# The first eight transfers of a kernel, spread over the queues of SyncE and ScalarE

## What is computed

```python
def rmsnorm(x, g):
    xf = x.astype(jnp.float32)
    y = xf * lax.rsqrt(jnp.mean(xf * xf, axis=-1, keepdims=True) + EPS)
    return (y * g.astype(jnp.float32)).astype(x.dtype)

def first_block(x, c, ada_w, ada_b, pre_mix_g, ...):
    c_act = jax.nn.silu(c)
    for l in range(DEPTH):
        mod = c_act @ ada_w[l] + ada_b[l]
        sh1, sc1, ga1, sh2, sc2, ga2 = [m[:, None, :] for m in jnp.split(mod, 6, axis=-1)]
        h = rmsnorm(x, pre_mix_g[l]) * (1.0 + sc1) + sh1
        y = hybrid_mixer(h, w_in[l], ...)
        x = x + ga1 * rmsnorm(y, post_mix_g[l])
        h = rmsnorm(x, pre_ffn_g[l]) * (1.0 + sc2) + sh2
        y = swiglu_ffn(h, w_ffn_in[l], w_ffn_out[l])
        x = x + ga2 * rmsnorm(y, post_ffn_g[l])
    return x
```

## Time and profile before

| | |
|---|---|
| median of 3 runs | 1330.96 us (1330.03 to 1331.42) |
| the profiled execution's own time | 1328.96 us |
| its span, first to last instruction | 1327.1 us |
| outside its span | 1.86 us |
| TensorE busy | 1309.0 us, 99% of the span |
| transfers | 155.60 MB, mean 117 GB/s, all the kernel's own on one hardware queue |

### The profile page before, as it was taken

The page is one execution under the profiler, slowest core; times in us unless marked ns, Lnnn a source line. Parts: engine busy times, 40 slices in busy tenths (PEclk is TensorE's granted clock), DMA queues, the critical chain, the costliest instruction groups (busy, mean ns, idle before and its releaser), DMA issues. The chain is left out here.

```text
span 1327.1 us, 19480 instructions
## 1 busy us (share of the span) xinstructions
PE 1309.0 (99%) x7546; PEld 1150.7 (87%) x7546; DVE 1045.7 (79%) x1317; ACT 731.6 (55%) x1045; POOL 113.2 (9%) x86
## 2 busy tenths in 40 slices
PE   8999999999999999999999999999999999999997
PEld 6889888879989989989999897888888898889886
DVE  7899999999989689746849769997577876786663
ACT  4424888785546345534545856787365434443444
POOL 0000000012100591000012001010200000000001
PEclk9999999999999999999999999999999999999999
DMA  9634411167333433222252151301222232223212
GB/s 366 256 128 112 159 63 48 33 220 277 131 149 104 143 143 122 101 96 96 96 191 72 64 175 48 93 27 64 96 95 95 95 100 91 95 95 128 77 69 76
DMA packets 28731, 155.60 MB, mean 117 GB/s; under 512 B 3248, under 2 KB 5680, under 8 KB 15600
## 3 DMA queue, kind: packets, MB, share of 16 engines
q1 hardware_dynamic: 28656, 154.58, 33.4%
HBM read 145.39 MB, written 4.19 MB: 113 GB/s over the span
## 5 line engine op out<-in xcount | busy, mean ns | idle before, releaser
L2155 DVE TENSOR_TENSOR w_lo<-raw,w_hi 128x2048 fp32r<-128x2048 f32 (+3 forms) x139 | 249.4, 1796 | 47.0 <-ACT w_hi L1237 35.3
L1237 ACT ACTIVATE w_hi<-raw 128x2048 fp32r<-128x2048 f32 (+2 forms) x74 | 131.2, 1773 | 31.3 <-PE psum L920 15.4
L658 PE MATMUL psum<-h_hi,w_hi 128*128 128x512 f32 x360 | 92.1, 394 | 0.1
L658 PE MATMUL psum<-h_hi,w_lo 128*128 128x512 f32 x360 | 91.1, 391 | 0.0
L658 PE MATMUL psum<-h_lo,w_hi 128*128 128x512 f32 x360 | 90.4, 389 | 0.0
L658 PE MATMUL psum<-xg_hi,w_hi 128*128 128x512 f32 x336 | 83.0, 389 | 0.0
L658 PE MATMUL psum<-xg_hi,w_lo 128*128 128x512 f32 x336 | 83.0, 389 | 0.0
L658 PE MATMUL psum<-xg_lo,w_hi 128*128 128x512 f32 x336 | 83.0, 389 | 0.0
L658 PEld LDWEIGHTS psum<-h_lo,w_hi 128*128 128x128 f32 x360 | 67.6, 188 | 14.1
L658 PEld LDWEIGHTS psum<-h_hi,w_lo 128*128 128x128 f32 x360 | 67.0, 188 | 13.7
L658 PEld LDWEIGHTS psum<-h_hi,w_hi 128*128 128x128 f32 x360 | 66.0, 188 | 14.2 <-DVE w_lo L2155 0.7
(11 more groups left out here) (501 smaller groups left out, 3336.7 us busy)
## 6 DMA issues: line engine op xcount, KB each, us to landing
raw<-w_ffn_in SPq DMA_DIRECT2D x22, 1024.0 KB, 4.9
raw<-w_up SPq DMA_DIRECT2D x22, 1024.0 KB, 4.8
ada_first<-ada SPq DMA_DIRECT2D x16, 512.0 KB, 12.0
raw<-w_gate SPq DMA_DIRECT2D x8, 1024.0 KB, 4.9
raw<-w_mix_out SPq DMA_DIRECT2D x8, 1024.0 KB, 4.9
raw<-w_ffn_out SPq DMA_DIRECT2D x8, 1024.0 KB, 4.9
raw<-w_down SPq DMA_DIRECT2D x8, 1024.0 KB, 4.8
ada_x<-ada SPq DMA_DIRECT2D x11, 512.0 KB, 5.3
```

Source lines behind the costliest of these rows:

```text
L658: last = mm(ps, w[slot][:, k, t * P:(t + 1) * P], part(xv, k0 + k), start=first, stop=final)
L1237: A(w_hi[slot][:, 0:stage.kc, :], raw[slot][:, 0:stage.kc, :], ACT.Copy).then_inc(sem["w_hi_done"], 1)
L2155: return tt(out_lo, full, high.bitcast(F32), ALU.subtract)
```

## The change

ScalarE's stream now begins with three transfers, issued before it loads its table: `small`, `ident` and the second quarter of `x`. SyncE's stream no longer issues those three; it begins with the first, third and fourth quarter of `x`. Semaphores and their counts are the same, and so is every other instruction.

```diff
-            sp.dma_start(small[:, :], dram["small"]).then_inc(sem["in_small"], 16)
-            sp.dma_start(ident[:, :], dram["mats"][:, 0, :]).then_inc(sem["in_ident"], 16)
-            for part in range(4):
+            for part in (0, 2, 3):
                 two = slice(2 * part, 2 * part + 2)
                 sp.dma_start(x[:, two, :], dram["x"][:, two, :]).then_inc(sem[f"x_ada{part}"], 16)
             sp.dma_start(vec[:, :], dram["vec"]).then_inc(sem["in_vec"], 16)
...
+            act.dma_start(small[:, :], dram["small"]).then_inc(sem["in_small"], 16)
+            act.dma_start(ident[:, :], dram["mats"][:, 0, :]).then_inc(sem["in_ident"], 16)
+            act.dma_start(x[:, 2:4, :], dram["x"][:, 2:4, :]).then_inc(sem["x_ada1"], 16)
             nc.scalar.preload_act_table_set("natural_log_exp_and_others")
             act.wait_ge(sem["in_small"], 16)
```

## The result

The changed kernel took 1332.36 us (median of 12 runs, 1330.72 to 1333.63), the kernel before 1330.26 beside it (12 runs): a ratio of 1.0018, 95% interval 1.001 to 1.0025, or 1.3 to 3.3 us slower. I had forecast 1330.5 us, within 1329.3 to 1332.0, and no change of 0.2% or more. The change is of that size (0.18%), but it is clear of no change and has the other sign: I had 0.5 us off. The profiled execution took 1333.33 us with a span of 1330.2. The time outside the span did not grow: its median is 1.8 us over the 12 executions, and 1.9 to 2.4 us over the four sets of executions of the kernel before that stand beside the experiments. So the loss lies within the span.

What follows compares the result with a forecast made beforehand. TensorE, 99% busy, bounds the kernel, hanging from the first `glu` matmul. Taking 0.5 us off gave a span of 1326.6; with 1.86 outside it, 1328.5, and 2.0 for the median, 1330.5 us, range 1329.3 to 1332.0.

Steps and rivals of the forecast that it cites:

- Two issues leave the front of SyncE's stream: Start of SyncE's stream: the first quarter of `x` is issued 0.93 us sooner, and no more is gained.
- ScalarE issues three transfers: ScalarE's start: three issues take 1.4 us, delaying L733 by 0.95, within 2.1 us of cover.
- the rival: Start: the two queues' issues take turns, gaining only 0 to 0.5 us, about 1330.8 us; chance 0.2.
- The constants now compete: Stream of `x`: sharing with `small` and `ident` trims the gain; last quarter and transfers behind come 0.6 us sooner.
- the constants crawl: Start: `ident` waits among packets of `x`; mildly 0.3 to 0.8 us lost (chance 0.1), heavily 9.3 (0.02).
- The second quarter rides beside the first: Loads of `x`: sharing engines, quarter 0 lands at 5.7; ScalarE's squares end at 10.0, 0.6 us sooner.
- VectorE: VectorE's adds and copy at the start: packed, the last add ends at 10.95, 0.45 us sooner.
- Sum: First `glu` matmul: 0.5 to 0.6 us sooner, taken as 0.5 us off the kernel.
- A second queue costs outside the span: Outside the span: a rival adding 1.86 us less the 0.5, giving 1332.3 us; chance 0.06.
- A loss of TensorE's clock: Gap before L733, about 0.7 us: a rival in which TensorE's clock falls; given no chance of its own.

Runs made afterwards that it cites:

- b: Second profile of the kernel that, against the kernel before, moves only `small` and `ident` to ScalarE's queue; this execution took 1332.22 us.

## Why the prediction was wrong, step by step

- *Two issues leave the front of SyncE's stream*: right. Quarter 0 was issued at 0.74 and landed 4.1 us later, as before; quarter 3 near 9.1, where I had 9.0.
- *ScalarE issues three transfers*: right in size (from 0.73 to 2.11, 1.38 us with the gaps; I took 1.4), table load at 2.14. That ScalarE's and SyncE's issues hinder each other, as the rival had it, was wrong here: 0.41 to 0.46 us each. The Trainium skill's lock on a shared descriptor generator ("Perfetto Trace Analysis", "DMA Instruction — HWDGE (DVE, Sync)") shows no delay in these rows.
- *The constants now compete*: **failed**. I priced them by their bytes, 0.2 to 0.5 us, charged to the stream. They took 1.8 us (`small`) and 2.5 us (`ident`) longer to land than before, because they pay by packets. The mild form of the rival *the constants crawl* had this (two to three microseconds), with 0.1 as its chance. Its price of 0.3 to 0.8 us was too high for an execution in which the clock holds: with the constants alone the copy began at 9.15 instead of 8.79, and the start was 0.08 late. By the median of that kernel, 2.0 us, it was too low.
- *The second quarter rides beside the first*: **failed**, and this is the step that made the sum wrong for the start. I let quarter 1 share from its issue on and land at 6.5 or sooner, with quarter 0 slowed to 5.7. But its queue is in order: it could not begin before the constants were through. Quarter 0 was not slowed (4.86), and quarter 1 landed at 8.94. Squares until 11.89 instead of 10.0 follow from that.
- *VectorE*: the packing was right and turned against the change. Add, copy and two adds take 3.0 us packed, as I had worked out, but behind the second square, which ended at 10.0 instead of 7.85: the last add ends at 13.05 instead of 10.95. The profile with the early copy confirms this part (0.65 us).
- *Sum*: the start moved by +1.56 us in the profile instead of by -0.5, more than the 1 us that I had named as the sign of being wrong. That the end follows the start was right in the means: 1.6 us of shift against 1.3 to 3.3 measured. Part of 2.1 us is left over (0.5 us), which two and three profiles don't resolve. The base was off too: I added to 1330.96, the median of three runs, where the 12 gave 1330.26; so the change was missed by 2.6 us, not by the 1.9 between the two times.
- *A second queue costs outside the span*: wrong; there are 1.8 us outside it now and 1.9 to 2.4 before.
- *A loss of TensorE's clock*: I gave it no chance, on a column read wrongly, and put its gap at 0.7 us where it was 1.76. The windows print 1.00 before the first change that the trace records. In the changed kernel, the same matmuls of ones took 234 ns a record at the start (4.21 / 18) and 119 ns later (2.62 / 22), with 1.00 printed for 1 to 3 us (columns as above):

```profile
1.06 4.21 PE L724 MATMUL psum<-ones 128*128 128x128 f32 x18 [1.06 <-DVE ones L2302]
...
14.33 2.62 PE L724 MATMUL psum<-ones 128*128 128x128 f32 x22
```
```profile
1.00:3.00 2.00, 1.94 (x9) 1.00 0.42 89
```

  So the clock is at 1.2 GHz at the start, and where two queues make the c matmuls late, behind an idle TensorE, it is low for part or all of them in 8 of 13 profiles (2.43 to 3.78 us; the kernel that waits for `ident` not counted), in neither of before's, and in none of the four with 18 matmuls of ones. It cost 1.4 us in b. It cost the changed kernel nothing: its starts of 17.85 and 17.98 are later by as much as its three squares, which began at 9.19 and 9.32 instead of 8.94, and the copy stood behind the late add there anyway.

Open, first: why the constants alone had a median 2.0 us above before, when three of their four profiles start at 16.1 (one fall of 1.4 in four doesn't make 2.0). The three are fast executions, with spans of 1327.2 to 1329.1; b has 1330.2. Of the eleven behind the median, five have spans of 1328.2 to 1329.4 and six of 1330.2 to 1331.7. A fall in about half of them would give such a median, but that is not shown. It bears on the whole: the five kernels measured over many executions that issue the constants from ScalarE's queue, with nine matmuls of ones, all have ratios above 1 (1.0009 to 1.0021; that with the third quarter touches 1.0), and the two that issue a quarter alone there have 0.9997. So what is shown of quarter 1 is its 1.5 us of start; by the medians, moving the constants alone loses as much as the whole change. Second: what makes the copy of `qkT` land 8.0 to 10.8 us after its issue. No version here is faster than the kernel before by more than the noise.

The Trainium skill's rule that issuing from several engines saves issue time and no more ("DMA: Bandwidth & Descriptors", "Issuing engines are not separate DMA queues") gave the right gain for quarter 0, 0.93 us, and would have had the kernel faster. The section "Queues, rings and completion order" of the same page has the turns: each DMA engine goes round the queues by packets, and takes a whole packet from one before it switches. The rows agree that the share goes by packets, with 97 against 96; how long a turn is they don't show.

## What to carry to other kernels

A transfer of many short rows can cost little while the engines are empty and much beside a transfer of long rows on another queue: here 12 KB in 128 rows landed 1.8 us later. In this kernel the constants did well ahead of the stream, on the same queue, and a large transfer that is needed early did badly behind them on a second queue while the first was full. When a stream is split over queues, work out in which order its parts land, not only when the last one does.

## What the runs showed that I had not expected

- One queue's 144 packets of `small`, 12 KB in all, took 3.5 us to land beside a stream of 4 KB rows, and 1.7 us without it.
- An idle gap of TensorE of 1.8 to 2.2 us ahead of the four c matmuls left them at 1.98 us in some executions and at 2.43 to 3.24 us in others of the same two kernels (the changed one, and the constants alone), the slower ones behind the longer gaps.
- The 512 KB copy within one kernel landed 8.0 to 10.8 us after issue, and an execution's time moved with it by 1.85 us at the same start: more than the change that was measured here.
